# Two halves of the tokens at the passages between the sublayers of a transformer kernel

## What is computed

```python
h = h + FFN_RES * rmsnorm(swiglu(rmsnorm(h, g[0]), gate, up, down), g[1])   # sublayers 0, 2, 3, 5
h = h + rmsnorm(mixer(rmsnorm(h, g[2])), g[3])                              # 1 and 4: attention
x = x + rms_norm(mixed @ w_out, g_mix_post)                                 # 6: attention and mLSTM
x = x + rms_norm(square(relu(rms_norm(x, g_mlp_pre) @ w_up)) @ w_down, g_mlp_post)   # 7
```

## Time and profile before

| | us |
|---|---|
| median of 3 runs | 1592.48 (1592.34 to 1601.32) |
| profiled execution, as a run | 1599.82 |
| its span in the profile | 1597.7 |
| TensorE busy | 1526.1 |
| VectorE, ScalarE, GpSimd busy | 935.3, 666.7, 168.2 |

### The profile page before, as it was taken

One profiled execution on the slowest core, in us unless ns is written; L12 is line 12 of the kernel. 1 busy time (PEld: TensorE's weight loads), 2 busy tenths in 40 slices (PEclk: granted clock), 3 DMA queues, 4 the chain that ended last, 5 costly groups with the idle time before them and its releaser, 6 DMA issues.

```text
span 1597.7 us, 27848 instructions
## 1 busy us (share of the span) xinstructions
PE 1526.1 (96%) x11578; PEld 1445.0 (90%) x11578; DVE 935.3 (59%) x1124; ACT 666.7 (42%) x827; POOL 168.2 (11%) x183
## 2 busy tenths in 40 slices
PE   6999989999899998999989998899998999899997
PEld 5999989968899998999989967899997987899996
DVE  5665465465766546665455465666646655777544
ACT  4443444434544434443433354444434333444432
POOL 1000029010300003000021000300003010210001
PEclk9999999999999999999999998999999987999998
DMA  7557854403355664554554401355555520355550
GB/s 222 163 181 182 221 184 159 134 28 95 114 168 177 182 192 148 167 183 141 167 168 157 160 1 35 125 185 184 167 179 160 179 94 1 106 159 184 185 185 27
DMA packets 250782, 233.55 MB, mean 146 GB/s; under 512 B 29759, under 2 KB 249844, under 8 KB 250688
## 3 DMA queue, kind: packets, MB, share of 16 engines
q1 hardware_dynamic: 250224, 231.96, 46.7%
q10 hardware_dynamic: 464, 0.25, 0.1%
HBM read 230.99 MB, written 1.12 MB: 145 GB/s over the span
## 4 chain that ended last, share of the span: by engine, by line
PE 85%; DVE 8%; ACT 2%; POOL 2%; issue 1%; DMA 1%; SPq 0%; POOLq 0%; DVEq 0%; ACTq 0%
PE acc L547 24%; PE acc L548 24%; PE acc L549 24%; DVE scaled L1360 3%; DVE rstd L1335 2%; PE aux L630 1%; PE aux L739 1%; PE aux L782 1%; POOL sq_sum L1932 1%; DVE w_lo L1330 1%; ACT w_hi L1004 1%; POOL h L1939 1%; PE acc L759 1%; DVE x_lo L1341 1%; PE aux L747 1%
## 5 line engine op out<-in xcount | busy, mean ns | idle before, releaser
L547 PE MATMUL acc<-x_hi,w_hi 128*128 128x272 f32 (+1 forms) x2432 | 701.6, 288 | 30.1 <-DVE x_lo L1341 21.6
L548 PE MATMUL acc<-x_lo,w_hi 128*128 128x272 f32 (+1 forms) x2432 | 697.1, 287 | 0.0
L549 PE MATMUL acc<-x_hi,w_lo 128*128 128x272 f32 (+1 forms) x2432 | 694.6, 286 | 0.0
L1330 DVE TENSOR_TENSOR w_lo<-raw,w_hi 128x2048 fp32r<-128x2048 f32 (+1 forms) x230 | 487.5, 2120 | 332.2 <-ACT w_hi L1004 332.2
L1004 ACT ACTIVATE w_hi<-raw 128x2048 fp32r<-128x2048 f32 (+1 forms) x230 | 406.0, 1765 | 410.1 <-PE acc L549 409.7
L547 PEld LDWEIGHTS acc<-x_hi,w_hi 128*128 128x128 f32 x2432 | 461.4, 190 | 39.9 <-issue 23.3
L548 PEld LDWEIGHTS acc<-x_lo,w_hi 128*128 128x128 f32 x2432 | 460.3, 189 | 0.4
L549 PEld LDWEIGHTS acc<-x_hi,w_lo 128*128 128x128 f32 x2432 | 460.4, 189 | 0.0
L547 PE MATMUL acc<-hid_hi,w_hi 128*128 128x272 f32 (+1 forms) x704 | 203.5, 289 | 0.0
L548 PE MATMUL acc<-hid_lo,w_hi 128*128 128x272 f32 (+1 forms) x704 | 201.5, 286 | 0.0
L549 PE MATMUL acc<-hid_hi,w_lo 128*128 128x272 f32 (+1 forms) x704 | 200.9, 285 | 0.0
(11 more groups left out here) (261 smaller groups left out, 1308.9 us busy)
## 6 DMA issues: line engine op xcount, KB each, us to landing
raw<-in_ffn_w_gate SPq DMA_DIRECT2D x44, 1024.0 KB, 5.3
raw<-in_ffn_w_up SPq DMA_DIRECT2D x44, 1024.0 KB, 5.4
raw<-in_ffn_w_down SPq DMA_DIRECT2D x32, 768.0 KB, 4.4
raw<-in_ffn_w_down SPq DMA_DIRECT2D x32, 640.0 KB, 4.3
raw<-in_w_up SPq DMA_DIRECT2D x16, 1024.0 KB, 5.4
raw<-in_w_down SPq DMA_DIRECT2D x16, 1024.0 KB, 5.1
raw<-in_na_w_qkv SPq DMA_DIRECT2D x12, 1024.0 KB, 5.1
raw<-in_da_w_qkv SPq DMA_DIRECT2D x12, 1024.0 KB, 5.1
```

Of the source, the lines that this page charges most:

```text
L547: nc.tensor.matmul(o, wh, xh, start=first, stop=False)
L548: nc.tensor.matmul(o, wh, xl, start=False, stop=False)
L549: return nc.tensor.matmul(o, wl, xh, start=False, stop=last)
L1330: nc.vector.tensor_tensor(w_lo[:, part, 0:nk * CW], raw[:, slot, 0:nk * CW], w_hi[:, part, 0:nk * CW].bitcast(F32), ALU.subtract).then_inc ...
```

## The change

**At the end of an output phase** the tokens are halved: 136 and 136 (128 and 128). In the last output group every panel runs as half matmuls. In its earlier panels (`half_panel`) each chunk is done for both halves in turn; in its last panel (`last_panel`), which has 8 chunks, all of the first half is done first, then all of the second, each in two quarters (m). The halves lie in different banks, acc and aux (`half_banks`). A mixer's group is one panel, which is that last one. `FFN_PARTS` becomes 3, 3, 8 and 8 chunks.

**Squares, sum, root, reciprocal, residual and x** are made per half (`boundary` on ScalarE, `residual` on VectorE), in units of a quarter for the squares and of two chunks for the residual. y gets its gain when the bank is emptied. The residual is added by VectorE (`add_pair`); GpSimd's `add_branch` goes, and it folds the two rows of sq_sum into one. The warming matmuls after an output phase go.

**At the start of an input phase** (`first_panels`) the first panel runs through all chunks on the first half, then the second panel; then both on the second half. The third panel goes into aux, and the norm's sum is made within it.

**Weights.** w_hi and w_lo get four slots; w_lo takes the place of raw in memory, so that a load waits until the panel four earlier was used. ScalarE makes w_hi as soon as raw is there. At the passage the next phase's first two panels are split ahead of it and the third and fourth between and after the pieces of x.

Semaphore counts follow these orders. The transposes at the end go through acc by token halves. The core of the diff:

```diff
 SLOTS = 4
-FFN_PARTS = ((0, 6), (6, 5), (11, 6), (17, 5))
+FFN_PARTS = ((0, 3), (3, 3), (6, 8), (14, 8))
...
+        w_lo = sb("w_lo", [P, SLOTS, FULL * CW], F32R, [cursor[0]])
         raw = sb("raw", [P, SLOTS, FULL * CW])
-        w_hi = sb("w_hi", [P, 2, FULL * CW], F32R)
-        w_lo = sb("w_lo", [P, 2, FULL * CW], F32R)
+        w_hi = sb("w_hi", [P, SLOTS, FULL * CW], F32R)
...
+        def banks(n, i, j):
+            if n % 2 == 0 and n > 0 and isinstance(i, int) and (i, j) == (0, 2):
+                return aux[:, 0:2, :]
+            return acc[:, j % 2, :, :]
+        def half_banks(part):
+            return aux[:, 0:2, :] if part else acc[:, 1, :, :]
...
-                wait(sp, w_lo_ready, p - 3)
+                wait(sp, panel_used, p - 3)
...
+                for part, half in enumerate(halves(tokens)):
                     for m in range(2):
-                        w = slice(q * CW + m * P, q * CW + m * P + P)
-                        mm = product(acc[:, pair, m, 0:rhs_hi.shape[2]], w_hi[:, slot, w], w_lo[:, slot, w],
-                                     rhs_hi[:, k, :], rhs_lo[:, k, :], first and q == 0,
-                                     last and q == len(chunks) - 1)
+                        for q, k in enumerate(chunks):
+                            if part == 1 and m == 0 and q == 4:
+                                sum_half(k_, 0, tokens)
+                            wait_rhs(k)
+                            w = slice(q * CW + m * P, q * CW + m * P + P)
+                            mm = product(half_banks(part)[:, m, half], w_hi[:, slot, w], w_lo[:, slot, w],
+                                         rhs_hi[:, k, half], rhs_lo[:, k, half], only and q == 0, q == len(chunks) - 1)
+                            if q == len(chunks) - 1:
+                                if part == 1 and m == 1:
+                                    mm.then_inc(panel_used, 1)
+                                else:
+                                    mm.then_inc(quarter_done, 1)
...
+                if free is not None:
+                    pe.wait_ge(acc_free, free)
+                for q, k in enumerate(chunks):
+                    for part, half in enumerate(halves(rhs_hi.shape[2])):
+                        mm = chunk(half_banks(part)[:, :, half], p % SLOTS, q, rhs_hi[:, :, half], rhs_lo[:, :, half], k,
+                                   first and q == 0, False)
                 mm.then_inc(panel_used, 1)
...
+            def first_panels(k_, tokens):
+                n = 2 * k_
...
+                for part, half in enumerate(halves(tokens)):
+                    for j in range(2):
+                        for k in range(DC):
+                            if part == 0 and j == 0 and k == 4:
+                                sum_half(k_ - 1, 1, tokens)
+                            if j == 0:
+                                pe.wait_ge(x_ready, SPLIT_IN[k_] + 8 * part + k + 1)
+                            if part == 0 and k == 0:
+                                pe.wait_ge(w_lo_ready, ph.p0 + j + 1)
+                                if j == 0:
+                                    pe.wait_ge(acc_free, ph.a0 - 1)
+                                else:
+                                    pe.wait_ge(quarter_out, 3 * k_ - 1)
+                            mm = chunk(banks(n, 0, j)[:, :, half], (ph.p0 + j) % SLOTS, k, x_hi[:, :, half], x_lo[:, :, half],
+                                       k, k == 0, k == DC - 1)
+                            if part == 1 and k == DC - 1:
+                                mm.then_inc(panel_used, 1)
...
+                else:
+                    first_panels(k_, tokens)
+                    one(0, 2, ph.a0, sums, at=3)
+                    one(0, 3, ph.a0 + 2)
...
+                for g in range(4):
+                    for j, (k0, nk) in enumerate(parts):
+                        if (g, j) == (3, 3):
+                            last_panel(k_, None, range(k0, k0 + nk), False, rhs_hi, rhs_lo, lambda k: None)
+                        elif g == 3:
+                            half_panel(n, j, ph.a0 + 2 if j == 0 else None, range(k0, k0 + nk), j == 0, rhs_hi, rhs_lo)
+                        else:
+                            panel(n, g, j, ph.a0 + g - 1 if j == 0 else None, acc[:, g % 2, :, :], range(k0, k0 + nk), j == 0,
+                                  j == 3, rhs_hi, rhs_lo, ready if g == 0 else lambda k: None)
...
+            def sum_half(k_, part, tokens):
+                half = halves(tokens)[part]
+                pe.wait_ge(sq_added, additions(2 * k_ + 1) + 3)
+                wait(pe, sd_ready, 3 * k_ + 1 + part)
+                pe.wait_ge(sq_ready, squares_before(2 * k_ + 1) + 5 + 2 * part)
+                nc.tensor.matmul(ps_half[:, half], ones[:, :], sq_sum[:, 0, half], start=True, stop=False)
+                nc.tensor.matmul(ps_half[:, half], ones[:, :], sq[:, 1, 0, half], start=False, stop=False)
+                nc.tensor.matmul(ps_half[:, half], ones[:, :], sq[:, 1, 1, half], start=False, stop=True)\
+                    .then_inc(sum_ready, 1)
...
-                sum_rest(2 * k + 1, tokens_out)
-                if k < 7:
-                    keep_warm(aux[:, 0, :], 18)
...
+            def high_part(k, part, c):
                 g0, _, _, tokens, _ = SUBS[k]
+                half = halves(tokens)[part]
+                act.wait_ge(h_ready, DC * k + 4 * part + c // 2 + 1)
+                nc.scalar.activation(x_hi[:, c, half], h[:, c, half], ACT.Copy,
+                                     scale=gains[:, g0 + c:g0 + c + 1]).then_inc(x_hi_ready, 1)
...
+            def boundary(k):
+                tokens = SUBS[k][4]
+                first, second = halves(tokens)
+                square_quarter(k, 0, 0)
+                square_quarter(k, 0, 1)
+                deviation(3 * k + 1, first)
+                square_quarter(k, 1, 0)
+                if k == MLP:
+                    square_quarter(k, 1, 1)
+                    deviation(3 * k + 2, second)
+                    return
+                for c in range(DC):
+                    high_part(k + 1, 0, c)
+                    if c == 1:
+                        square_quarter(k, 1, 1)
+                deviation(3 * k + 2, second)
+                n = 2 * k + 2
+                for c in range(DC):
+                    high_part(k + 1, 1, c)
+                    if c % 2:
+                        high(n, 0, 2, c // 2, 4)
+                for pair in range(4):
+                    square(n, pair, h[:, 2 * pair:2 * pair + 2, 0:tokens], tokens)
+                high(n, 0, 3)
+                deviation(3 * k + 3, slice(0, tokens))
+                if k + 1 not in (NA, DA, MIX, MLP):
+                    load_table(ACT.Silu)
...
-                    if (local + 1) % groups_of == 0:
...
-                    if local + 1 == PHASES[n].panels:
-                        deviation(2 * k + 1, tokens)
-                    split_ahead(n, i, j)
+                    if local <= last - 2:
+                        high(n, i, j + 2)
+                    if local == last - 2 and k < MLP:
+                        high(n, i, j + 3)
+                        high(n, i, j + 4)
+                    if local == last:
+                        boundary(k)
...
+            def add_pair(k, part, q):
+                half = halves(SUBS[k][4])[part]
+                width = half.stop - half.start
+                c = slice(2 * q, 2 * q + 2)
+                r = rstd[:, 1, half].unsqueeze(1).broadcast_to([P, 2, width])
+                done = 8 * k + 4 * part + q
+                nc.vector.tensor_tensor(y[:, c, half], y[:, c, half], r, ALU.mult).then_inc(scaled_ready, 1)
+                dve.wait_ge(scaled_ready, done + 1)
+                nc.vector.tensor_tensor(h[:, c, half], h[:, c, half], y[:, c, half], ALU.add).then_inc(h_ready, 1)
...
+                first, second = halves(SUBS[k][4])
+                quarter_y(k, 0, 0)
+                quarter_y(k, 0, 1)
+                dve.wait_ge(quarter_out, 3 * k + 2)
+                reciprocal(3 * k + 1, first)
+                quarter_y(k, 1, 0)
+                for q in range(4):
+                    add_pair(k, 0, q)
+                    if q == 2:
+                        quarter_y(k, 1, 1)
+                    if q >= 1 and k < MLP:
+                        low_part(k + 1, 2 * q - 2, 0)
+                        low_part(k + 1, 2 * q - 1, 0)
                 dve.wait_ge(acc_free, PHASES[2 * k + 1].a0 + 4)
-                reciprocal(2 * k + 1, tokens)
...
+                reciprocal(3 * k + 2, second)
+                for q in range(4):
+                    add_pair(k, 1, q)
+                    if k < MLP:
+                        if q == 0:
+                            low_part(k + 1, 6, 0)
+                            low_part(k + 1, 7, 0)
+                        else:
+                            low_part(k + 1, 2 * q - 2, 1)
+                            low_part(k + 1, 2 * q - 1, 1)
```

(69 more changed lines are left out.)

362 lines of the change are left out of this document (176 added, 186 removed).

## The result

| | before | after |
|---|---|---|
| median, us | 1592.41 (1591.36 to 1601.32) | 1794.86 (1787.42 to 1798.35) |
| ratio | 1 | 1.1251, 95% interval 1.1197 to 1.1305 |
| span of the profiled execution | 1597.7 | 1785.6 |
| mean granted clock of TensorE | 0.979 | 0.937 |

The change makes the kernel 202 us slower; forecast were 114 (1706 us, at most 1748). The direction was right and the size was not.

The account below looks back on a forecast made before the run. The prediction took TensorE, busy 96% of the span, as the bound. Halves +158.9, passages -65.6, tail -4.5 and cut +25 gave +114 us on 1592.5, so 1706 us, with a range of 1620 to 1748 (8 in 10).

Parts of the forecast that it names:

- A half costs 0.112 us: Last output groups and first two input panels: 1536 matmuls become 3072 halves, each paced by its weight load, +158.9 us.
- The price of 81 ns: Skill's figure for a load and 128-column matmul; would make the halves' term +63.6 us, time near 1615; not adopted.
- The passages: Seven passages between sublayers: waits and sums of 107.4 us before shrink to 41.8 in all, -65.6 us.
- the 1.65 of the sum: First input panel after a passage: VectorE needs 1.65 us per pair of chunks, TensorE 1.35.
- a passage keeps 3.3 us of wait: First input panel, first token half: ends at 15.5 instead of 12.2, as x comes late from VectorE.
- they lay inside the wait and cost nothing: The 18 warming calls behind output phases: removing them was costed at nothing.
- The cut: FFN down panels of 3, 3, 8, 8 chunks: waits of 3.0 + 3.2 us in each of four FFNs, +25 us.
- Tail: End of the kernel after the last output matmul: 11.8 us instead of 15.4 + 0.9, -4.5 us.
- Queues: Panel loads on SP and a new wait on ScalarE in mixer output phases: both costed at nothing.
- Sum: Whole kernel: 158.9 - 65.6 - 4.5 + 25 = +114 us, giving 1706 us.
- its rivals: Halves costing their columns, 1580 us (0.13); free cut, 1681; less passage gain, 1733; f32 pace, about 2045 (0.05).

## Why the prediction was wrong in size

**A half costs 0.112 us** (+158.9): right. 30.29 us for 272 instructions is 0.111, and the run with 200 columns shows that the columns don't set it. The price of 81 ns for a load and a matmul of 128 columns that the Trainium skill gives ("TensorE: Matmul & The Clock Gate", section "Back-to-back issue gap") isn't met by these four-byte weights.

**The passages** (-65.6): right where the clock held. The two half panels of the first passage take 24.4 us, 192 x 0.112 = 21.5 and 2.9 of waits and sums beyond; forecast were 3.3 and 0.7, so some 1.1 more a passage. VectorE's step for two chunks took 1.37 us (249.79 to 251.16) against the 1.65 of the sum. The third panel's norm wait is 0.54, forecast 0.5.

**The clock**: the step that failed. Every pace in the sum came from rows at a granted clock of 1.00, and the step "a passage keeps 3.3 us of wait" costed the wait at its own length. In its place the runs showed a wait of 1.8 us that at five of seven passages is followed by 34 to 38 us at 1.2 GHz, halves of 0.213 us each but for the last 2.5 to 5.2 us: 88.7 us. The profile before had the sign: it fills its own waits with 18 unread matmuls, and the change takes them away ("they lay inside the wait and cost nothing"). I priced what they cost and not what they hold. Still, in the kernel on whole tokens they hold little (3.3 us), so looking at them alone wouldn't have given the size.

**The cut** (+25): a wait of 3.1 at the start and three of 0.7 to 1.1 us behind it, 5.8 per FFN against 6.2 (the page's 17.7 for four counts idle time alone), so the term as I defined it was right. As the price of that part of the change it was not: taking it back is worth some 9.5 us with the clock held, and nothing that two executions show without. The step left out the clock here too. Behind the wait at the start of each of the four down phases it falls, amid 272 or 256 columns for 3.4 us only, with about 1.5 us lost each time (15 matmuls at 0.227 instead of 0.125 us):

```profile
165.10:168.50 3.40, 3.40 (x17) 3.40 (x16) 3.05 (x2) 1.16 (x2) 0.00 (x0) 0.50 0.83 204
```

**Tail** (-4.5): from the last output matmul to the end 9.8 us (1775.8 to 1785.6) against 15.4, -5.6 with the sums left aside.

**Queues** (0): SyncE's and ScalarE's order cost nothing that shows. VectorE's did: one w_lo behind GpSimd's masks, 7.4 us, not foreseen. Before, w_lo came through the same stream in 2.3 to 2.9 us each time, and no row said that it might not.

**Sum**: 158.9 - 65.6 - 5.6 + 4 x 5.8 + 7.4 = +118, and +88.7 for the clock: 1799, measured 1794.9. As the 88.7 is itself the difference of two medians, this checks the other terms alone, at 1711 against 1706; the short falls (+6) and the smaller passages (-8) about cancel. No case of the prediction, in its range up to 1748 or among its rivals, had this one in it: all were about the price of a half and of the waits, each at full clock.

**What stays open.** At two of the seven passages (249.5 and 686.5 us) the clock holds behind the same wait of 1.84 us. They follow FFNs, as do two at which it falls. No run tells what decides between them, nor whether the narrow matmuls before the wait or those behind it bring the long fall. Why w_lo got through GpSimd's stream before and not after wasn't settled either; only that gaps in the stream let it through.

**A version that beats both** is the one on whole tokens with spread masks: 1561.8 us, 1.9% below the kernel before (1.5 to 2.2). What it has over the kernel before are the change's other parts (four slots and early splits, the residual on VectorE alone, the third panel in aux), shared chunks with x made chunk by chunk, and the moved sums; no run takes these apart.

## What to carry over

A wait is worth its length only while the clock holds: where load-bound, narrow matmuls stand around it, fill it or walk the loops so that it doesn't arise, and check the granted clock of that stretch before anything else. Splitting a matmul's tokens in two doubles its weight loads. Here a half with its load took 0.112 us and the whole matmul 0.125, so each split nearly doubled the price (+158.9 us), and the 9.4 us of waits per passage that the halves were to give back (-65.6) don't buy it back. When a part of a change seems to have a price, ask what it covers, and try the parts apart: here the halves lost and the rest won.

## What the hardware showed

- Float32r matmuls of 128, 136 or 200 columns, each with its own load of 128 weight columns, start 0.112 us apart at 2.4 GHz; with 128 or 136 it is 0.213 at 1.2 GHz, so this pace slows with the clock. With 272 columns it is 0.125 and 0.227.
- A wait of 1.8 us between half matmuls brought 34 to 38 us at 1.2 GHz at five of seven passages, until 2.5 to 5.2 us after whole-width matmuls had begun again; with 200 columns instead of 128 or 136 it brought none. 43.4 us of the same half matmuls without a wait stayed at 2.4 GHz, and so did the passages in which eight unread matmuls filled the wait. Waits of 4.8 to 6.3 us with 272 or 256 columns around them brought 3.4 or 6.8 us. That an idle TensorE loses its clock agrees with the Trainium skill ("TensorE: Matmul & The Clock Gate", section "Part 1: The HAM clock gate"), with these waits as the case. What these runs add is the short wait between half matmuls, and that the clock stayed down while they ran on without a gap.
- VectorE's subtraction of two SBUF tiles waited for a whole stream of GpSimd additions, 10.17 and 17.88 us instead of 2.3. The Trainium skill ("SBUF — State Buffer", section "Who interferes with whom") says that a VectorE instruction with two SBUF inputs contends with a GpSimd instruction that reads SBUF, over a shared port pair that one of them locks. The trace agrees that one waits for the other, but here VectorE came through only after 11 and 22 further instructions of GpSimd, and in the kernel before it was through in 2.3 to 2.9 us each time.
